# Router logits from the raw rows, with the first norm folded into the router's matrix

## The reference, cut to what matters

```
y = hybrid_mixer(h, ...)                       # ends in  [rms(o_dil)*g_dil, rms(o_fox)*g_fox] @ w_out
h = layer_norm(ALPHA * h + y, ln1_g, ln1_b)    # (x - mu) * rsqrt(var + eps) * g + b
logits = h @ w_router + b_router               # 16 columns
probs = softmax(logits)                        # 4 groups of 4: best group, its two best experts
gates = the two probabilities / their sum
y = sum over the two experts of gate * (silu(h @ w_gate) * (h @ w_up)) @ w_down
h = layer_norm(ALPHA * h + y, ln2_g, ln2_b)
```

## Time and profile before

| | us |
|---|---|
| median of 3 runs (lowest, highest) | 1366.09 (1365.68, 1370.46) |
| the profiled execution's own time | 1370.7 |
| its span, first to last instruction | 1369.0 |
| mean granted clock of PE | 0.908 of full speed |
| PE busy | 1122.7 (82%) |
| DVE busy | 312.4 (23%) |
| ACT busy | 182.1 (13%) |
| read from HBM | 443 MB, mean 325 GB/s |

### The profile page before, as it was taken

One profiled execution on the slowest core, in us unless ns is written; L12 is line 12 of the kernel. 1 busy time (PEld: TensorE's weight loads), 2 busy tenths in 40 slices (PEclk: granted clock), 3 DMA queues, 4 the chain that ended last, 5 costly groups with the idle time before them and its releaser, 6 DMA issues.

```text
span 1369.0 us, 17057 instructions
## 1 busy us (share of the span) xinstructions
PE 1122.7 (82%) x6068; PEld 571.9 (42%) x6069; DVE 312.4 (23%) x791; ACT 182.1 (13%) x373; POOL 4.6 (0%) x12
## 2 busy tenths in 40 slices
PE   7999877799977768679799975999998876577775
PEld 5776443344433233224577644445443332222232
DVE  0443531111111111112254443001111111111113
ACT  2233210001000100001223320100000100000100
POOL 0000000000000000000000000000000000000000
PEclk9999878899988899789899986999999998778888
DMA  9814319899999999999931430656989999999994
GB/s 367 360 62 164 143 44 426 350 419 428 429 428 428 429 428 429 429 428 423 419 135 62 185 143 13 246 199 264 383 326 374 429 429 428 428 428 428 428 429 204
DMA packets 34712, 444.83 MB, mean 325 GB/s; under 512 B 4080, under 2 KB 4336, under 8 KB 5872
## 3 DMA queue, kind: packets, MB, share of 16 engines
q1 hardware_dynamic: 33520, 440.08, 77.6%
q0 software_dynamic: 1152, 4.19, 0.8%
HBM read 443.22 MB, written 1.05 MB: 325 GB/s over the span
## 4 chain that ended last, share of the span: by engine, by line
PE 61%; DMA 29%; issue 6%; DVE 3%; SPq 1%; ACT 0%; DVEq 0%; ACTq 0%
DMA ring<-in_w_up_dram 23%; PE lo L566 13%; PE lo L670 9%; PE lo L554 9%; PE acc L453 8%; DMA ring<-in_w_down_dram 6%; PE acc L431 5%; PE lo L541 3%; PE acc L529 3%; PE acc L622 1%; PE lo L836 1%; PE acc L505 1%; PE lo L493 1%; PE acc L729 1%; PE lo L529 1%
## 5 line engine op out<-in xcount | busy, mean ns | idle before, releaser
L566 PE MATMUL lo<-ring,work 128*32 128x512 f32 x2112 | 276.0, 671 | 150.7 <-DMA ring<-in_w_up_dram 131.4
L566 PEld LDWEIGHTS lo<-ring,work 128*32 128x32 f32 x2112 | 68.2, 121 | 339.0 <-issue 164.0
L554 PE MATMUL lo<-ring,work 128*64 128x512 f32 x672 | 153.0, 611 | 26.4 <-issue 23.5
L541 PEld LDWEIGHTS lo<-work,h 128*128 128x128 f32 x1088 | 130.2, 193 | 53.8 <-issue 49.7
L541 PE MATMUL lo<-work,h 128*128 128x128 f32 x1088 | 146.6, 285 | 2.5 <-DVE work L1266 2.5
L670 PE MATMUL lo<-ring,work 128*128 128x512 f32 x288 | 126.8, 601 | 15.8 <-issue 15.8
L453 PE MATMUL acc<-actT,ring 128*128 128x256 f32 x512 | 119.2, 388 | 0.0
L453 PEld LDWEIGHTS acc<-actT,ring 128*128 128x128 f32 x512 | 98.6, 195 | 14.7 <-issue 1.6
L554 PEld LDWEIGHTS lo<-ring,work 128*64 128x64 f32 x672 | 48.3, 140 | 125.9 <-issue 116.6
L670 PEld LDWEIGHTS lo<-ring,work 128*128 128x128 f32 x288 | 55.2, 193 | 84.7 <-issue 84.7
L1324 DVE TENSOR_TENSOR work<-lo,work 64x512 f32<-64x512 f32 x22 | 15.0, 682 | 291.8 <-ACT work L1008 291.8
(11 more groups left out here) (183 smaller groups left out, 691.8 us busy)
## 6 DMA issues: line engine op xcount, KB each, us to landing
ring<-in_w_gate_dram SPq DMA_DIRECT2D x64, 2048.0 KB, 12.9
ring<-in_w_up_dram SPq DMA_DIRECT2D x64, 2048.0 KB, 18.7
ring<-in_w_down_dram SPq DMA_DIRECT2D x64, 2048.0 KB, 24.1
ring<-in_w_in_dram SPq DMA_DIRECT2D x24, 1024.0 KB, 25.0
ring<-in_w_out_dram SPq DMA_DIRECT2D x8, 1024.0 KB, 29.5
ln_gb<-in_ln_dram POOLq DMA_DIRECT2D x8, 512.0 KB, 7.0
cst<-in_consts_dram SPq DMA_DIRECT2D x1, 1544.0 KB, 17.9
h<-in_x_dram SPq DMA_DIRECT2D x1, 1024.0 KB, 5.2
```

The source lines that it names most:

```text
L541: mm = nc.tensor.matmul(lo[:, 2 + k // 4, (k % 4) * P:(k % 4 + 1) * P], h[:, t, k * P:(k + 1) * P], place_t[:, t], start=(k % 4 == 0 and t ...
L554: mm = nc.tensor.matmul(lo[half * W:(half + 1) * W, bank, :], lhsT, ring[:, s, at:at + 512], start=start, stop=stop, skip_group_check=True)
L566: return nc.tensor.matmul(lo[at * T:(at + 1) * T, bank, :], lhsT, ring[:, s, col:col + 512], start=start, stop=stop, skip_group_check=True)
```

## The change

Four things change; the loops over experts stay.

1. The logits are taken from the raw rows (before the norm). With wr_ln = g * w_router, logits = (raw @ wr_ln - mu * sum(wr_ln)) / std + (sum(b * w_router) + b_router). `fold_norm` makes `wr_ln` and the two column sums at the front of the layer, on DVE; one more matmul in `sum_decay` adds them over the partitions, and `take_totals` keeps them. The raw rows get a buffer of their own (the place of `v_tok`). The softmax's shift is by a minimum of the negated logits, and its sum and division are gone.
2. The order at the end of attention: block 0's forgetting part is multiplied before block 1's last dilated part, so that block 0's statistics and turning stand beside block 1's products.
3. The norm is split into `norm_stats` and `norm_apply`. `seed` follows the logits.
4. Ranks and counts are separate sums with separate semaphores; the gate table is made after the plan.

```diff
+        raw = work[:, 0:2048].rearrange("p (t c) -> p t c", t=TB)
...
+            def turn_raw(t, banks, release=None):
+                for b in range(2):
+                    for i in range(4):
+                        k = 4 * b + i
+                        mm = nc.tensor.transpose(banks[b][:, i * P:(i + 1) * P], raw[:, t, k * P:(k + 1) * P], ident)
+                        if release is not None and k == 0:
+                            mm.then_inc(release, 1)
+                    mm.then_inc(turned, 1)
+            def logits(t, ks):
+                for k in ks:
+                    mm = nc.tensor.matmul(lo[:, 1 - t, 0:NEXP], actT[:, k, t * P:(t + 1) * P],
+                                          wr_ln[:, k, :], start=(k == 0), stop=(k == KB - 1), skip_group_check=True)
+                if ks[-1] == KB - 1:
+                    mm.then_inc(logits_done, 1)
...
+                pe.wait_ge(fold_ready, l + 1)
+                nc.tensor.matmul(acc[:, 0, P + SEQ:P + SEQ + 2 * NEXP], ones, wr_sum[:].rearrange("p a e -> p (a e)"),
+                                 start=False, stop=True, skip_group_check=True).then_inc(cum_done, 1)
...
-                mix(l, 1, (2, 3), x_banks[1], 0, 5, fulls)
+                mix(l, 1, (2,), x_banks[1], 0, 5, fulls)
                 weigh_values(l, 7)
+                mix(l, 1, (3,), x_banks[1], 0, 5, fulls)
+                pe.wait_ge(sq_added, 6 * l + 6)
+                sum_squares(1)
+                pe.wait_ge(dil_taken, l + 1)
+                mix(l, 0, (6, 7), y_banks[0], 6, 7, fulls).then_inc(proj_done, 1)
                 mix(l, 1, (4, 5), x_banks[1], 0, 5, fulls).then_inc(dil_done, 1)
-                pe.wait_ge(sq_added, 6 * l + 6)
-                sum_squares(1, ring_free[ODD + 2])
-                for t in range(TB):
-                    pe.wait_ge(dil_taken, TB * l + t + 1)
-                    mix(l, t, (6, 7), y_banks[t], 6, 7, fulls).then_inc(proj_done, 1)
-
+                pe.wait_ge(raw_ready, 2 * l + 1)
+                turn_raw(0, (acc[:, 0, :], lo[:, 1, :]), ring_free[ODD + 2])
+                mix(l, 1, (6, 7), y_banks[1], 6, 7, fulls).then_inc(proj_done, 1)
+                pe.wait_ge(actT_act, 8 * l + 6)
+                logits(0, first_half)
+                pe.wait_ge(raw_ready, 2 * l + 2)
+                turn_raw(1, y_banks[1], ring_free[ODD + 3])
+                logits(0, second_half)
+                pe.wait_ge(actT_act, 8 * l + 8)
+                logits(1, range(KB))
                 for t in range(TB):
                     pe.wait_ge(h_ready, 4 * l + 3 + t)
-                    turn_block(h, t, ring_free[ODD + 3] if t == 0 else None)
-                for t in range(TB):
-                    pe.wait_ge(actT_act, 8 * l + 6 + 2 * t)
-                    for k in range(KB):
-                        mm = nc.tensor.matmul(lo[:, 0, t * NEXP:(t + 1) * NEXP], actT[:, k, t * P:(t + 1) * P],
-                                              wr[:, k, :], start=(t == 0 and k == 0), stop=(k == KB - 1),
-                                              skip_group_check=True)
-                mm.then_inc(logits_done, 1)
-                seed(0)
-                seed(1)
+                    seed(t)
                 pe.wait_ge(sel_ready, l + 1)
-                nc.tensor.matmul(lo[:, 1, 0:NEXP], tri0[:, 0:P], sel[:, 0, :], start=True, stop=True,
-                                 skip_group_check=True)
-                for at, mats in ((NEXP, (ones, tri0[:, 0:P])), (2 * NEXP, (ones, ones))):
-                    for t in range(TB):
-                        mm = nc.tensor.matmul(lo[:, 1, at:at + NEXP], mats[t], sel[:, t, :], start=False,
-                                              stop=(t == 1), skip_group_check=True)
-                mm.then_inc(ranks_done, 1)
+                both = sel[:].rearrange("p t e -> p (t e)")
+                nc.tensor.matmul(lo[:, 0, 0:2 * NEXP], tri0[:, 0:P], both, start=True, stop=False, skip_group_check=True)
+                nc.tensor.matmul(lo[:, 0, NEXP:2 * NEXP], ones, sel[:, 0, :], start=False, stop=True,
+                                 skip_group_check=True).then_inc(ranks_done, 1)
+                for t in range(TB):
+                    mm = nc.tensor.matmul(lo[:, 1, 0:NEXP], ones, sel[:, t, :], start=(t == 0), stop=(t == 1),
+                                          skip_group_check=True)
+                mm.then_inc(counts_done, 1)
...
-                roots(l, 0)
-                copy_turned(l, 1, range(4))
+                ln_root_of(l, 0, 0)
+                copy_turned(l, 1, 0, (acc[:, 0, :], lo[:, 1, :]))
+                copy_turned(l, 1, 1, (lo[:, 2, :], lo[:, 3, :]))
+                ln_root_of(l, 0, 1)
                 a.wait_ge(shifted, l + 1)
-                nc.scalar.activation(rt[:, 1], rt[:, 0], ACT.Exp).then_inc(router_exp, 1)
+                nc.scalar.activation(rt[:, 1], rt[:, 0], ACT.Exp, scale=-1.0).then_inc(router_exp, 1)
...
+            def fold_norm(l):
+                for i, scale in ((1, ln1_b), (0, ln1_g)):
+                    step(nc.vector.tensor_tensor(wr_ln[:], wr, scale.unsqueeze(2).to_broadcast([P, KB, NEXP]), ALU.mult))
+                    op = nc.vector.tensor_reduce(wr_sum[:, i, :], wr_ln[:].rearrange("p k e -> p e k"), AX.X, ALU.add)
+                    if i:
+                        step(op)
+                op.then_inc(fold_ready, 1)
+            def take_totals():
+                at = P + SEQ
+                nc.vector.tensor_copy(wr_tot[:, 0, :], acc[:, 0, at:at + NEXP])
+                nc.vector.tensor_tensor(wr_tot[:, 1, :], acc[:, 0, at + NEXP:at + 2 * NEXP], br[:, 0, :], ALU.add)
...
+                fold_norm(l)
                 v.wait_ge(cum_done, l + 1)
+                take_totals()
...
-                v.wait_ge(dil_done, 2 * l + 2)
-                for half, bank in enumerate((acc[:, 1, :], lo[:, 0, :])):
-                    at = slice(half * 512, (half + 1) * 512)
-                    op = nc.vector.scalar_tensor_tensor(out=h[:, 1, at], in0=bank, scalar=rms[:, 2, 0, 1:2],
-                                                        in1=h[:, 1, at], op0=ALU.mult, op1=ALU.add)
-                step(op)
-                v.sem_inc(dil_taken, 1)
                 mean_squares(l, 1)
+                y_of = (acc_tok[:, 1, :], lo_flat[:, 1024:2048])
                 for t in range(TB):
                     v.wait_ge(proj_done, 2 * l + t + 2)
-                    step(nc.vector.scalar_tensor_tensor(out=h[:, t, :], in0=acc_tok[:, 1 - t, :],
-                                                        scalar=rms[:, 2, 1, t:t + 1], in1=h[:, t, :],
-                                                        op0=ALU.mult, op1=ALU.add))
-                    layer_norm(l, 0, t, h[:, t, :])
+                    nc.vector.scalar_tensor_tensor(out=raw[:, t, :], in0=y_of[t], scalar=rms[:, 2, 1, t:t + 1],
+                                                   in1=h[:, t, :], op0=ALU.mult, op1=ALU.add).then_inc(raw_ready, 1)
+                    v.wait_ge(raw_ready, 2 * l + t + 1)
+                    norm_stats(l, 0, t, raw[:, t, :])
+                    if t == 0:
+                        v.wait_ge(dil_done, 2 * l + 2)
+                        for half, bank in enumerate((acc[:, 1, :], lo[:, 0, :])):
+                            at = slice(half * 512, (half + 1) * 512)
+                            op = nc.vector.scalar_tensor_tensor(out=h[:, 1, at], in0=bank, scalar=rms[:, 2, 0, 1:2],
+                                                                in1=h[:, 1, at], op0=ALU.mult, op1=ALU.add)
+                        step(op)
+                    norm_apply(l, 0, t, raw[:, t, :])
+                for t in range(TB):
+                    v.wait_ge(logits_done, 2 * l + t + 1)
+                    step(nc.vector.scalar_tensor_tensor(out=rt[:, 0, t, :], in0=wr_tot[:, 0, :], scalar=mv[:, t, 0:1],
+                                                        in1=lo[:, 1 - t, 0:NEXP], op0=ALU.mult, op1=ALU.subtract))
+                    step(nc.vector.scalar_tensor_tensor(out=rt[:, 2, t, :], in0=rt[:, 0, t, :],
+                                                        scalar=lnt[:, 2, t:t + 1], in1=wr_tot[:, 1, :], op0=ALU.mult, op1=ALU.subtract))
+                step(nc.vector.tensor_reduce(r2[:, 0], rt[:, 2], AX.X, ALU.min))
...
-                step(nc.vector.tensor_reduce(r2[:, 1], rt[:, 1], AX.X, ALU.add))
-                step(nc.vector.reciprocal(r2[:, 2], r2[:, 1]))
-                step(nc.vector.tensor_tensor(rt[:, 2], rt[:, 1], r2[:, 2].unsqueeze(2).to_broadcast([P, TB, NEXP]),
-                                             ALU.mult))
...
                 v.wait_ge(ranks_done, l + 1)
...
                 for t in range(TB):
                     nc.vector.tensor_scalar(place_t[:, t, 0:W], iota[:, 0:W], rank_tab[:, t, 0:1], None, ALU.is_equal)
+                v.wait_ge(counts_done, l + 1)
+                step(nc.vector.tensor_scalar(wide_shift[:], lo[:, 1, 0:1], W + 0.5, float(W), ALU.is_gt,
```

(15 more changed lines are left out.)

72 lines of the change are left out of this document (37 added, 35 removed).

## The result

The changed kernel took 1346.03 us (median of 4 runs, 1344.52 to 1349.40) beside 1368.28 for the kernel before in the same session (4 runs, 1365.68 to 1370.85). The ratio of the changed kernel's time to the other's is 0.9846, interval 0.9821 to 0.9871. A second session, here called the control, gave 1346.42 (5 runs, 1344.71 to 1349.73), ratio 0.9843, interval 0.9812 to 0.9874. The forecast was 1347.5, with 1350.4 for the span.

The account below looks back on a forecast made before the run. The router stage, with the load stream waiting for the first item, was taken as the bound. 9.80 + 0.74 - 0.25 = 10.3 us a layer, less 1.0 for the clock, 18.6 in both, gave 1347.5; range 1340 to 1355.

Parts of the forecast that it names:

- What bounds it: Router stage of each layer: loads stand still until the first item, so starting it earlier moves all that follows equally.
- Block 0's forgetting product first: End of attention: block 0's product ends 3.44 us earlier, so DVE begins block 0 at 154.62 in layer 0.
- DVE as the bound, PE done 0.7 before it: Before the ranks: PE's logits end at 167.7, 0.7 us before DVE ends block 1's norm at 168.41.
- Rank sums: From selection to the gather: split sums take 1.85 us instead of 2.59, 0.74 gained a layer.
- Hidden edits: Folding, about 1.3 us, hides in DVE's idle layer front; gate table hides behind the plan; softmax's 0.65 us is saved.
- The clock: Turning, logits and gather: a falling PE clock costs zero to 3.9 us a layer; 1.0 was taken off.
- (a): Clock low from early in turning and logits and again for the gather: 12.8 us gained in both layers, 1353.3; chance 0.26.
- From sum to time: Whole program: 18.6 us off the profiled 1370.7 gives 1352.1; the median, 4.6 lower, is predicted at 1347.5.
- (b): First item of each layer also starts warm, up to 2.9 us more gained in each: 1341.7; chance 0.08.
- (c): The load stream sets the end regardless and the gain is given back, leaving 1366; chance 0.06.
- (d): PE's code placement moves and later items wait longer for issue: 37 us lost, 1384; chance 0.03.
- 16.8: Gain in both layers, 2 x 8.4 us, if the gather after PE's idle time starts cold, losing 1.9 in each.

Follow-up runs that it names:

- the delay run: Changed kernel with ten 512-column copies added on DVE between the first placement and the plan in each layer: 1359.60 us, ratio 0.9927.
- the second kernel with POOL: Changed kernel with block 1's last norm operation on POOL as multiply and add, plus products of constants on PE between gather and first item: 1353.36 us, ratio 0.9879.

## Why the prediction was right, point by point

- **What bounds it.** Right. The router stage is paid in full and a microsecond there is one at the end: 10.47 and 20.84 at the two first items, 21.3 at the end; the delay experiment says at least as much from the other side.
- **Block 0's forgetting product first.** Predicted start of DVE 154.62, measured 154.75. The difference is the 0.12 by which the extra matmul moved PE at the front (44.36 to 44.48); I had put 0.25 for it.
- **Block 1's raw row.** Predicted 162.66, measured 162.42: turning took 0.87 from its start to the next product's (157.91 to 158.78), not 1.04, and k = 6, 7 took 3.44, not 3.55.
- **DVE as the bound, PE done 0.7 before it.** Right. Logits end at 167.54 (predicted 167.7), DVE begins on them at 168.07 (168.41). The room that counts is larger than this difference, because DVE first corrects block 0: it wants block 1's logits at 168.61, and takes them 0.11 after their end where it waits for them (167.41 to 167.52 in the delay run), so the room is 0.96. Logits longer by 1.64 (4.49) therefore brought the ranks 0.68 later there.
- **Ranks.** Predicted 169.99, measured 169.85: the operations before them took 0.2 more than my 1.58, the norm 0.1 less.
- **Rank sums.** Predicted a gain of 0.74, measured 0.54 (2.78 to 2.24, both from `sel` to the gather). From the end of `sel` to the gather it is 2.05, where I had counted 1.85. The form is worth 0.68 when undone alone.
- **Hidden edits.** The front hides the folding (half of it done again is hidden too), and the gate table is free: it stands behind the plan, and the item begins 4.16 after the plan as before. The softmax's 0.65 was exact.
- **The clock.** Here a term was mis-sized. I took 1.0 off each layer and the runs took nothing off: 10.47 and 10.56 a layer, where the sum without the allowance is 10.3 (and 10.5 with the terms as measured). The logits kept the full clock in both layers of both profiles of this kernel (24 of them in 2.85 each time). That nothing came off is in part luck: in the delay run, whose code before the ranks is the same, the clock fell in layer 0, for 0.68. With almost the whole stretch cold (old order, layer 0, 6.30 from the turning to the last logits, where I had reckoned 6.9) it was 1.57, so the 2.0 was of the right size for that case. The seeds ran at the lower level in layer 0, but ended at 172.8, before `sel`, so the mean clock from 162 to 171 was 0.81, just over the 0.8 expected. A gather at the lower level cost nothing. Rival (a) priced it at 1.9, since I let the whole issue of 4 us start after the gather's end; a gather of 6.74 showed that it doesn't.
- **From sum to time.** The forecast median stood 1.5 above the measured one; the profiled execution 2.7 above its counterpart (1352.1, 1349.4). The allowance of 2.0 is most of it. That the median came closer than the profiled pair is chance: I started from 1366.1, and from the 1368.28 measured beside the changed kernel the same subtraction gives 1349.7. A spread of the same size exists between executions of one kernel: 1344.5 to 1349.7, of which 2.5 us at the front of layer 0.
- **The rivals.** (a) did not happen: the gather was partly cold in the control and in layer 1, but not the logits, and its 1.9 for the gather was never paid. (b) did not happen by itself in the first profile (10.03, still cold at 0.50 from 185.3 on) and in part in the control (8.77); forced in layer 0 it did not move the median. In layer 1 the first item is of another kind (up to 128 tokens), so the 2.9 had no ground there. (c) is refuted by the delay run. (d) was not seen: from plan to first item it is 4.16 and 10.68 (4.15 and 10.69 before), and the items behind took as long as before (458.97 in layer 0 to the last norm, 458.78 before; 518.7 from layer 1's first item to the end, 519.2 before).

The Trainium skill, page "TensorE: Matmul & The Clock Gate", section "HAM oscillation — how this bites in real kernels", says that products in short bursts, with waits for data longer than the burst between them, start cold each time. By the gathers this case's traces agree only in part. Where PE had idled 2.50 before the rank sums (layer 1) the gather took 5.39; where longer seeds (5.38) had filled that time but for 0.81 (layer 0) it took 3.84; yet in the control, behind seeds of 5.38 and a wait of 0.80 again, it took 5.34. With the old order a wait of 1.87 stood before turning and logits in both layers, and the turning took 1.37 in one and 1.09 in the other. What decides was not found. The prediction's 16.8 from this rule was too low for another reason: the gather is off the path, warm or cold.

**What each part is worth**, of 10.5 a layer: undone alone, the raw rows cost 6.4 to 6.6, the order 5.3 in layer 0 (3.2 and 2.1) and 3.9 in layer 1 (3.0 and 0.9), the softmax 0.65, the rank sums 0.68. In layer 0 their sum is over 10.5. I take it that order and raw rows share the warm and early logits, and that both edits made the seeds end after `sel`; no run separates this.

## What to carry to other kernels

When a stage runs with the memory at rest, look for what its critical product truly needs: here the router's logits needed the sums, not the normed rows, and a norm that is linear after its two statistics can be folded into a small matrix once per layer, hidden at the front. Count the room between the two engines that then run side by side, at the operation that really needs the other's result; here it was 0.96 us, and so logits longer by 1.64 cost 0.68. And before pricing a cold matmul stage, find what releases the next step: a cold gather cost nothing, since the plan releases the item; cold seeds cost nothing in the changed kernel, where they end before `sel`, and 0.56 to 0.92 in three others where they ended after it.

## What the runs showed of the hardware that was not expected

- Beside POOL's work on 128x1024 fp32 (2.84 for the multiply, 2.34 to 2.41 for the add) single small operations of DVE were stretched, and not all: the one that began with the multiply took 1.11 or 1.12 instead of 0.23, and one beside the add 2.11 or 2.43 instead of 0.29, to about the add's end. Six others beside the multiply in layer 1 (starting from 805.51 to 806.97) kept their 0.19 to 0.29. In the changed kernel, with ACT, PE and a load at work beside them, the stretched ones took 0.23 and 0.29.
- The granted clock can fall inside narrow matmuls though PE has no gap: the same 24 logits, behind the same turning of 1.09 with 0.58 of wait before it, took 2.85 in layer 0 of the kernel with constants behind the gather and 4.49 in layer 0 of the delay run. What decides between the two was not found.
- PE's 4 us before an item, which the profile calls issue, lie beside matmuls still running (the gather of 6.74, the eight products of 3.70). They are a delay counted from the plan, not from PE's last matmul, as long as PE is done by then: in the second kernel with POOL the products ended at 188.40 and the item began at 188.33, 4.95 after the plan.
- Executions of one kernel differ through the clock in two stretches at its front (8.84 or 7.15, 5.41 or 3.72), with PE busy throughout. That is 3.4 us, of which 2.5 were left at block 1's raw row, since the second execution had entered the first of them 0.85 later (24.30, 23.45).
